# Two paired attentions: value products moved one pair later, new slots for the weight tiles, a new place for the sums' inversion

## What is computed

```python
# A: three groups of 8 heads of 64, dilated windows (window 128, 512, 2048; dilation 1, 4, 16)
m = max(sc); p = exp(sc - m); l = sum(p)          # sc masked by the window
o = einsum('znhqk,znkhd->znqhd', p / l, vw); lse = m + log(l)
wts = softmax(stack(lses)); oa = einsum('gbsh,gbshd->bshd', wts, stack(outs))
# B: grouped-query attention, 8 query heads over 2 key heads of 64
sc = einsum('bqkgd,bskd->bkgqs', qc, kb_) * (HEAD_DIM ** -0.5)
p = softmax(sc, axis=-1); o = einsum('bkgqs,bskd->bqkgd', p, vb_)
```

## Time and profile before

| what | value |
|---|---|
| time, median of 3 runs | 2059.45 us (2058.76 to 2061.29) |
| the profiled execution: its own time | 2062.16 us |
| its span, first to last instruction | 2060.4 us |
| mean granted TensorE clock | 0.989 |
| TensorE products busy | 1998.9 us (97%) |
| DVE busy | 1148.9 us (56%) |
| ScalarE busy | 827.0 us (40%) |
| attention A, L619's first to the first `stat` product after it | from 1367 us to 1592 us |
| attention B | from 1625 us to 1747 us |

### The profile page before, as it was taken

How to read it: one execution, slowest core, us unless ns; L and a number is a source line. 1 busy time by engine, 2 the same in 40 slices (tenths; PEclk the granted TensorE clock), 3 DMA queues, 4 the chain that set the end, 5 groups by cost and what they waited for, 6 DMA issues and landing times.

```text
span 2060.4 us, 28688 instructions
## 1 busy us (share of the span) xinstructions
PE 1998.9 (97%) x10858; PEld 1626.4 (79%) x10858; DVE 1148.9 (56%) x1374; ACT 827.0 (40%) x1191; POOL 11.4 (1%) x21
## 2 busy tenths in 40 slices
PE   6999999999999999999999998999999999999997
PEld 4887788888887887788888886897777766788886
DVE  5855775555445856775555445536664634343444
ACT  4444433333223344433333223234445555544352
POOL 2000000000000000000000000000000000000000
PEclk8999999999999999999999999999999999999999
DMA  6212033332224212133333223523332112232221
GB/s 173 81 44 82 24 109 93 102 95 88 92 92 120 83 29 77 42 102 90 93 102 97 97 82 85 161 67 93 92 108 66 62 52 65 80 113 78 86 92 61
DMA packets 236731, 177.76 MB, mean 86 GB/s; under 512 B 11835, under 2 KB 231225, under 8 KB 236239
## 3 DMA queue, kind: packets, MB, share of 16 engines
q1 hardware_dynamic: 235664, 174.74, 28.5%
q10 hardware_dynamic: 430, 1.43, 0.3%
q0 software_dynamic: 528, 0.12, 0.1%
HBM read 167.88 MB, written 2.10 MB: 82 GB/s over the span
## 4 chain that ended last, share of the span: by engine, by line
PE 92%; DVE 4%; ACT 2%; DMA 1%; issue 1%; ACTq 0%; DVEq 0%; SPq 0%
PE ps L859 25%; PE ps L861 24%; PE ps L860 24%; PE ps L619 2%; PE ps L643 2%; PE ps L632 2%; PE ps L1246 1%; PE ps L1248 1%; PE ps L1247 1%; PE ps L1101 1%; PE ps L499 1%; PE ps L474 1%; PE ps L896 1%; PE ps L792 1%; PE ps L898 1%
## 5 line engine op out<-in xcount | busy, mean ns | idle before, releaser
L859 PE MATMUL ps<-h_hi,w_hi 128*128 128x512 f32 x1408 | 566.5, 402 | 2.5 <-ACT qk L1514 2.0
L861 PE MATMUL ps<-h_hi,w_lo 128*128 128x512 f32 x1408 | 552.5, 392 | 0.0
L860 PE MATMUL ps<-h_lo,w_hi 128*128 128x512 f32 x1408 | 548.6, 390 | 0.0
L1923 DVE TENSOR_TENSOR w_lo<-w_raw,w_hi 128x2048 fp32r<-128x2048 f32 (+3 forms) x110 | 227.1, 2065 | 236.5 <-ACT w_hi L1521 230.5
L859 PEld LDWEIGHTS ps<-h_hi,w_hi 128*128 128x128 f32 x1408 | 265.1, 188 | 62.7 <-issue 7.6
L861 PEld LDWEIGHTS ps<-h_hi,w_lo 128*128 128x128 f32 x1408 | 264.6, 188 | 60.9
L860 PEld LDWEIGHTS ps<-h_lo,w_hi 128*128 128x128 f32 x1408 | 265.0, 188 | 57.0 <-issue 2.2
L1521 ACT ACTIVATE w_hi<-w_raw 128x2048 fp32r<-128x2048 f32 (+3 forms) x108 | 186.7, 1729 | 232.4 <-PE ps L861 211.5
L2299 DVE TENSOR_TENSOR w_lo<-w_raw,w_hi 128x1024 fp32r<-128x1024 f32 (+1 forms) x118 | 126.5, 1113 | 193.5 <-ACT w_hi L1770 192.7
L859 PE MATMUL ps<-hid_hi,w_hi 128*128 128x512 f32 x352 | 138.7, 394 | 0.0
L861 PE MATMUL ps<-hid_hi,w_lo 128*128 128x512 f32 x352 | 138.0, 392 | 0.0
(11 more groups left out here) (397 smaller groups left out, 2812.3 us busy)
## 6 DMA issues: line engine op xcount, KB each, us to landing
w_raw<-in_ffn_w_up_dram SPq DMA_DIRECT2D x88, 512.0 KB, 4.5
w_raw<-in_w_in_dram SPq DMA_DIRECT2D x41, 1024.0 KB, 5.3
w_raw<-in_w_in_dram SPq DMA_DIRECT2D x32, 512.0 KB, 5.2
w_raw<-in_ffn_w_down_dram SPq DMA_DIRECT2D x32, 512.0 KB, 3.9
w_raw<-in_w_out_dram SPq DMA_DIRECT2D x12, 1024.0 KB, 5.3
w_raw<-in_ffn_w_down_dram SPq DMA_DIRECT2D x16, 384.0 KB, 3.3
swapped<-qk SPq DMA_DIRECT2D x96, 64.0 KB, 2.0
w_raw<-in_w_mem_kv_dram SPq DMA_DIRECT2D x4, 1024.0 KB, 5.1
```

Of the source, the lines that this page charges most:

```text
L859: pe.matmul(dst, lh, rh, start=first and j == 0, stop=False)
L860: pe.matmul(dst, lh, rl, start=False, stop=False)
L861: ins = pe.matmul(dst, ll, rh, start=False, stop=last and j == len(order) - 1)
L1923: dve.tensor_tensor(w_lo[:, slot, 0:n], w_raw[:, slot, 0:n], w_hi[:, slot, 0:n].bitcast(F32), ALU.subtract).then_inc(sem("w_split"), 1)
```

## The change

TensorE: `values(p-1)` now runs in pair p, between `turn(p, 0)` and `scores(p+1)`, with the slot 3p behind both; before, `values(p)` stood behind slot 3p+1 of its own pair. The last `values` stands behind the last slot, ahead of the last `factor`. `factor` waits for the copy of the last transpose too. ScalarE: the copy of a transpose with e = 0 waits for `values(p-1)`, which reads the buffer that it overwrites; A no longer has `between`, so a tile's copy in slot 3p+1 stands behind both exponentials of the next pair. DVE: `scale` runs one pair later; `invert` stands ahead of the masks in A (as before) and behind the maxima in B. `SLOT_A` is new, its first tile runs ahead of pair 0 (`lead_tiles`). In B, DVE's and ScalarE's part of the slots 11, 23 and 35 moves to 12, 24 and 36 (`KEPT_B`).

```diff
             def factor(h):
                 pe.wait_ge(sem("pair_inv"), upto(pe, "pair_inv", hbase + h + 1))
+                pe.wait_ge(sem("pt_copied"), upto(pe, "pt_copied", base + 2 * RES * (h + 1)))
...
             for p in range(PAIRS):
                 turn(p, 0)
-                slot(3 * p)
+                if p == 1 and ready is not None:
+                    ready()
+                if p:
+                    values(p - 1)
                 if p + 1 < PAIRS:
                     scores(p + 1)
+                slot(3 * p)
                 turn(p, 1)
                 slot(3 * p + 1)
-                if p == 0 and ready is not None:
-                    ready()
-                values(p)
-                if p % RES == RES - 1:
+                if p % RES == RES - 1 and p + 1 < PAIRS:
                     factor(p // RES)
                 slot(3 * p + 2)
+            values(PAIRS - 1)
+            factor(RES - 1)
...
             def copy(p, e):
                 n = pairs[p].width
                 act.wait_ge(sem("pt_done"), upto(act, "pt_done", base + 2 * p + e + 1))
+                if p and e == 0:
+                    act.wait_ge(sem("pair_pv"), upto(act, "pair_pv", RES * hbase + p))
...
-        def pair_dve(dve, pairs, bank, inv, norm, fill={}):
+        def pair_dve(dve, pairs, bank, inv, norm, fill={}, early=False):
...
-                if p and p % RES == 0:
+                if early and h and p % RES == 0:
                     invert(h - 1)
                 reduce(p, 0)
                 reduce(p, 1)
+                if not early and h and p % RES == 0:
+                    invert(h - 1)
+                if h and p % RES == 1:
+                    scale(h - 1)
                 slot(3 * p - 2)
-                if p and p % RES == 0:
-                    scale(h - 1)
                 slot(3 * p - 1)
                 slot(3 * p)
...
-        SLOT_A = [(0, 0, 1, 2, 2, 3, 4, 4, 5, 6, 6, 7), range(8, 20), range(20, 32),
-                  (32, 33, 34, 35, 36, 37, 39, 40, 42, 43, 45, 46)]
+        SLOT_A = [(-1, -1, 0, 0, 1, 1, 3, 3, 4, 4, 6, 6), (7, 7, 9, 10, 11, 12, 13, 15, 16, 16, 18, 18),
+                  (19, 19, 21, 22, 23, 24, 25, 27, 28, 28, 30, 30), (31, 31, 34, 35, 36, 37, 39, 40, 42, 43, 45, 46)]
...
         SLOT_B = dict(zip(SLOTS_B, UNITS_B))
+        KEPT_B = {i + (i % 3 == 2): u for i, u in SLOT_B.items()}
...
+            def lead_tiles():
+                tile2(2 * C2_V + 11, "t")
+                for part in range(2):
+                    next_tile(0, 0, part)
...
-                    lead=partial(tile2, 2 * C2_V + 11, "t"), ready=values_copied, roped={RES * hp: 6 * hp + 6 for hp in range(4)})
+                    lead=lead_tiles, ready=values_copied, roped={RES * hp: 6 * hp + 6 for hp in range(4)})
...
-            pair_act(act, a_pairs(), A_BANKS, prob2, prob2_t, norm_a, between=True, lead=partial(copy_values, 11),
+            def lead_copies():
+                copy_values(11)
+                copy_qk(1, 0)
+
+            pair_act(act, a_pairs(), A_BANKS, prob2, prob2_t, norm_a, lead=lead_copies,
...
-            pair_dve(dve, a_pairs(), A_BANKS, inv_a, norm_a,
+            pair_dve(dve, a_pairs(), A_BANKS, inv_a, norm_a, early=True,
```

More of the change, by code:

```diff
@@ L1832, in _ @@
             pair_act(act, b_pairs(), B_BANKS, prob_b, prob_bt, norm_bt, lead=partial(merge_copy, 0, C2_MA, 1),
-                     fill=slots(*[(i, partial(merge_copy, 0, C2_MA, k)) for i, (k, part) in SLOT_B.items() if part != 0]))
+                     fill=slots(*[(i, partial(merge_copy, 0, C2_MA, k)) for i, (k, part) in KEPT_B.items() if part != 0]))
             act.preload_act_table_set("silu_and_others")
@@ L2411, in _ @@
             pair_dve(dve, b_pairs(), B_BANKS, inv_b, norm_bt,
-                     fill=slots((0, partial(split2, C2_MA + 2)), *[(i, partial(merge, 0, C2_MA, k)) for i, (k, part) in SLOT_B.items() if k % 4 > 1],
-                                *[(i, partial(split2, C2_MA + k // 2 + 2)) for i, (k, part) in SLOT_B.items() if k % 2 and part != 0]))
+                     fill=slots((0, partial(split2, C2_MA + 2)), *[(i, partial(merge, 0, C2_MA, k)) for i, (k, part) in KEPT_B.items() if k % 4 > 1],
+                                *[(i, partial(split2, C2_MA + k // 2 + 2)) for i, (k, part) in KEPT_B.items() if k % 2 and part != 0]))
             split2(C2_MQ)
```

## The result

The changed kernel takes 2066.32 us in the median of 8 runs (2065.09 to 2066.67); the kernel before, run beside it, 2060.68 (2058.76 to 2064.55). The ratio is 1.0024, 95% interval 1.0014 to 1.0034: slower by 4.9 us by the ratio, 5.6 by the medians. Forecast was no change, 2060.1, with a range that ended at 2064.4. The profiled execution has a span of 2064.8 us against 2060.4, and an own time of 2066.67.

What follows compares the result with a forecast made beforehand. TensorE was taken as the bound, busy 1998.9 of 2060.4 us. Dilated attention +2.3 and grouped attention -1.7 us summed to +0.6; on the median of 2059.45 that gave 2060.1 us, range 2054.9 to 2064.4.

Steps and rivals of the forecast that it cites:

- The clock falls: Three new TensorE gaps of 2.5 us each bring half clock, 1.7 us each: 2065.2 us, slower; chance 0.12.
- Part 1: Both attentions, value products one pair later beside scores: 14 fewer array-shape changes at 0.15 us, -2.1 us in each.
- V to S is free: Both attentions: going from value products straight to scores costs nothing, 4.2 us lower, 2055.9 us; chance 0.07.
- Part 2: Dilated attention, new slots for weight tiles through bank 0: waits for their copies fall from 3.7 to 3.0 us, gain 0.7.
- Part 3: Dilated attention: late ropes delay masks, exponentials and tile copies; TensorE waits 2.6 us in pairs 3 and 7, +5.1 us.
- the rope is in time: Dilated attention: the swap lands earlier or a slot is misplaced, so Part 3 is 0: 2055.0 us, faster; chance 0.17.
- Part 4: Grouped attention: pair 4's transpose wait goes, -2.0 us; pair 5 waits for its exponential behind DVE's split, +2.4 us.
- fourth rival: Grouped attention: the transpose copy's new wait for value products binds, 0.3 us in 14 pairs: 2064.3 us, slower; chance 0.08.

Runs made afterwards that it cites:

- e_busy: Changed kernel plus twenty unread TensorE products in each wait of pairs 3 and 7 of the dilated attention; 2062.43 us, ratio 1.0012.
- e_rope: Changed kernel with DVE's ropes of slots 9 and 21 one slot later, behind the masks; 2059.15 us, ratio 0.9995; run again, 2060.16 us, ratio 0.9997.
- e_split: Changed kernel with DVE's split of slot 12 in the grouped attention one slot later, behind pair 5's maxima; 2063.65 us, ratio 1.0016.
- e_best: Changed kernel with the moves of e_rope and e_split, plus four tiles' copies in the grouped attention behind the first transpose's copy; 2055.68 us, ratio 0.9975.
- e_between: Changed kernel with the tile's copy between the two exponentials again in the dilated attention; 2062.75 us, ratio 1.0015.
- e_ropebetw: Changed kernel with the edits of e_rope and e_between together; 2062.21 us, ratio 1.0007.
- e_mode: Changed kernel with the moves of e_rope and e_split, plus a whole-array product ahead of 15 score groups in the dilated attention; 2062.74 us, ratio 1.0012.

## Why the forecast was wrong, point by point

**The step that failed** is the clock. The prediction held it at 1.00 in its likeliest case, and made "The clock falls" a rival with 0.12 that decides for slower "from the third on". It fell behind both gaps of A, for 1.5 us each (forecast 1.7), and e_busy shows that this is the gap's doing. The rows had both answers in them: 2.18 us of idle with a fall behind it, 1.97 without. The new gaps were forecast at 2.6 and 2.6: longer than the one that brought a fall. The trace of the kernel before also holds two gaps of the very size forecast, outside A and B, and both have a half clock behind them. One, of 2.50 us, ends at 839.00, and the clock is at half from 839.70 on. The other, of 2.46 us, ends at 1303.47; its wait and the window behind it:

```profile
PE ps L859 <- DVE w_lo L2299: 2.5, 1, 2.5
1303.90:1307.30 3.40, 3.40 (x18) 3.40 (x17) 3.23 (x6) 0.00 (x0) 0.00 (x0) 0.50 1.06 347
```

By the nearest rows the fall belonged into the sum, and at the prediction's own 1.7 the forecast would have been 2060.1 + 2 x 1.7 = 2063.5, or with B's gap of 2.4 too, 2065.2. I took a row that agreed once and one that disagreed once for an open question, without asking on which side of them the new gaps lie.

A smaller part of the distance is the base: the prediction stands on a median of 2059.45 (3 runs), and the kernel before measured 2060.68 beside the changed one. That is 1.2 of the 6.2 us between 2060.1 and 2066.32.

The Trainium skill (TensorE: Matmul & The Clock Gate, Why this matters for your kernels), whose warning of idle gaps between bursts was cited for this rival, is about longer gaps than these. That idle gaps bring the clock down, the traces of this case confirm, and they decide on the size: here it fell behind 2.46 and 2.49 us.

**Part 1 was right.** Forecast -2.1 and -2.1, measured -2.3 and -2.1, as what the other terms leave: 14 fewer changes at 0.15 to 0.165. V's last product to S's first takes 0.203 us in all 14 pairs of A, the value forecast. The rival that V to S is free is out. The Trainium skill (TensorEngine Tiling (Array Packing), Key Properties) has TensorE drain when the tiling mode changes. The traces fit: 0.20 us start to start from T to V, V to S and T to S against 0.11 between transposes, and 0.33 from F to V or S against 0.23 within F.

**Part 2 was too hopeful by 0.5.** Nine waits behind T, as counted, but where two F precede the T they cost 0.43 each by starts, where one does 0.34. The 0.33 taken for all was the idle time of a row of the second kind.

**Part 3 was right in mechanism and size**: late ropes in pairs 3 and 7 only, 2.5 us of idle each against 2.6, removed by moving these two ropes (e_rope), which also shows that ropes as late in pairs 1, 2, 6 and 10 cost nothing (DVE waits 4.4 to 5.2 us for their swaps there, and no wait of TensorE follows). The rival that the rope is in time is out.

**Part 4 was right on its one large term** (2.14 us for the exponential against 2.4, removed by e_split) and missed a small one: pair 1's second transpose now waits 0.46 us, because ScalarE runs a tile's copy (0.60 us) and the rounding of half a chunk ahead of the copy that it waits for.

```profile
1646.18 1.15 ACT L1784 ACTIVATE w_hi<-w_raw 128x512 fp32r<-128x512 f32 x2
1647.24 0.58 ACT L696 ACTIVATE prob_bt<-ps 128x512 f32<-128x512 f32 x1
1647.96 0.63 PE L632 MATMUL ps<-cm,prob_b 128*128 128x128 f32 x4 [0.46 <-ACT prob_bt L696]
```

V ended at 1646.44, in the middle of the rounding, so it is not the copy's new wait for V that binds, and e_best, which moves this tile's copy and rounding, removes the 0.46. The fourth rival, a wait for V in 14 pairs, is out. The waits of pairs 9 and 14 grew from 0.80 to 0.95.

**In sum**, with the clock at the price that its own rows gave, the same working would have said longer by 4.0 us for two falls, 5.7 for three. Measured were 4.9 with two falls: each was 0.2 cheaper than that, and 1.4 us of waits came on top (0.5 in part 2, 0.3 in part 3, 0.6 in part 4), less 0.2 more gain in part 1.

## What to carry to other kernels

In an engine's queue written out by hand, an operation that waits for a DMA or for a slow cast must not stand ahead of the short operations that the critical chain needs: two ropes and one split in the wrong slots of DVE's list turned a gain of 4 us into a loss of 5. Price an idle gap of TensorE by the nearest gap in the same trace, with what follows it: here a wait of 2.5 us costs 4. And when a product is added to measure something, count its instructions in the profile first.

## What was not expected of the hardware

The same gap does not always bring the clock down. Behind B's wait of 2.1 us it fell in the profiles of e_rope, e_rope_again, e_between and e_ropebetw, and held in those of the changed kernel and e_busy; behind the gaps of 2.5 us in A it fell in all four cases (changed kernel and e_split); behind waits of 1.5 us (e_between, e_ropebetw) and less inside A and B it never did. Outside them a shorter gap is no safety: in the kernel before a half clock begins at 221.89, and the gaps just ahead of it are 0.57 and 0.99 us. Each fall in A and B cost 1.5 to 1.6 us. And a change of shape delays more than the next product: in e_mode the second instruction behind it still starts 0.10 us late (0.213 instead of 0.111), so the delay to the first start alone undervalues it.
